# Two adaLN products and their turns move ahead of most of the second tile's first chunks, with identity matmuls between the chunks

## The reference, cut to what matters

```
mod = silu(c) @ w_ada + b_ada             # (1024 x 6144), one row for the prompt, 8 for the samples
shift1, scale1, gate1, shift2, scale2, gate2 = split(mod, 6)
h = rms_norm(x, g_norm1) * (1 + scale1) + shift1
z = h @ w_in                              # one projection of 1024 to 5712 columns
... two attention mixers, gates, w_o_a, w_o_b, w_out, a second norm, and an MLP of width 4096
```

## Time and profile before

| | |
|---|---|
| median of 3 runs | 958.31 us (956.93 to 959.46) |
| profiled execution, its own time | 959.45 us |
| its span, first to last instruction | 957.6 us |
| PE busy | 931.5 us (97%) |
| DVE, ACT, POOL busy | 497.5, 396.5, 140.5 us |
| mean granted TensorE clock | 0.985 of full speed |

### The profile page before, as it was taken

How to read it: one execution, slowest core, us unless ns; L and a number is a source line. 1 busy time by engine, 2 the same in 40 slices (tenths; PEclk the granted TensorE clock), 3 DMA queues, 4 the chain that set the end, 5 groups by cost and what they waited for, 6 DMA issues and landing times.

```text
span 957.6 us, 19787 instructions
## 1 busy us (share of the span) xinstructions
PE 931.5 (97%) x7510; PEld 852.7 (89%) x7510; DVE 497.5 (52%) x1178; ACT 396.5 (41%) x829; POOL 140.5 (15%) x140
## 2 busy tenths in 40 slices
PE   8889999999999999999999999999999999999997
PEld 7588678778888878998799999999999999999997
DVE  2563668964735688742157666444323354442332
ACT  3254646664666756433233434343212143332111
POOL 4200232141244665300000000000000000000000
PEclk9789999999999999999999999999999999999999
DMA  9636683454423555777323611333333333333312
GB/s 318 209 90 193 170 278 95 146 166 131 145 78 120 166 183 154 240 224 242 111 67 89 176 45 45 89 88 91 106 90 88 88 88 89 95 99 90 88 44 90
DMA packets 176233, 124.54 MB, mean 130 GB/s; under 512 B 14739, under 2 KB 152019, under 8 KB 176164
## 3 DMA queue, kind: packets, MB, share of 16 engines
q1 hardware_dynamic: 176034, 123.50, 42.6%
q10 hardware_dynamic: 130, 0.10, 0.0%
HBM read 116.99 MB, written 6.59 MB: 129 GB/s over the span
## 4 chain that ended last, share of the span: by engine, by line
PE 85%; DVE 5%; issue 4%; ACT 2%; POOL 1%; DMA 1%; SPq 0%; POOLq 0%; ACTq 0%; DVEq 0%
PE bank L978 24%; PE bank L979 23%; PE bank L980 22%; PE bank L1053 2%; PE bank L1076 2%; PE bank L1032 2%; PE bank L1062 2%; PE bank L881 1%; PE bank L1094 1%; DMA vbuf<-in_cache_v_a 1%; PE bank L903 1%; PE bank L1038 1%; PE bank L1117 1%; DVE sel L1997 1%; PE bank L1107 1%
## 5 line engine op out<-in xcount | busy, mean ns | idle before, releaser
L978 PE MATMUL bank<-h_hi,w_hi 128*128 128x256 f32 (+1 forms) x1232 | 360.9, 293 | 7.2 <-DVE h_lo L1876 6.5
L979 PE MATMUL bank<-h_lo,w_hi 128*128 128x256 f32 (+1 forms) x1232 | 351.4, 285 | 0.0
L980 PE MATMUL bank<-h_hi,w_lo 128*128 128x256 f32 (+1 forms) x1232 | 350.9, 285 | 0.0
L978 PEld LDWEIGHTS bank<-h_hi,w_hi 128*128 128x128 f32 x1232 | 235.9, 191 | 30.4 <-issue 21.4
L979 PEld LDWEIGHTS bank<-h_lo,w_hi 128*128 128x128 f32 x1232 | 235.8, 191 | 0.0
L980 PEld LDWEIGHTS bank<-h_hi,w_lo 128*128 128x128 f32 x1232 | 235.2, 191 | 0.0
L978 PE MATMUL bank<-u_hi,w_hi 128*128 128x264 f32 (+1 forms) x512 | 145.0, 283 | 0.0
L979 PE MATMUL bank<-u_lo,w_hi 128*128 128x264 f32 (+1 forms) x512 | 144.7, 283 | 0.0
L980 PE MATMUL bank<-u_hi,w_lo 128*128 128x264 f32 (+1 forms) x512 | 144.5, 282 | 0.0
L2414 DVE TENSOR_TENSOR w_lo<-raw,w_hi 128x1024 fp32r<-128x1024 f32 x58 | 71.1, 1226 | 132.9 <-ACT w_hi L1752 132.9
L1752 ACT ACTIVATE w_hi<-raw 128x1024 fp32r<-128x1024 f32 x58 | 61.3, 1056 | 139.8 <-PE bank L980 139.8
(11 more groups left out here) (328 smaller groups left out, 1375.8 us busy)
## 6 DMA issues: line engine op xcount, KB each, us to landing
raw<-in_w_in SPq DMA_DIRECT2D x44, 512.0 KB, 4.1
part<-in_w_ada SPq DMA_DIRECT2D x32, 512.0 KB, 5.8
raw<-in_w_up SPq DMA_DIRECT2D x32, 512.0 KB, 4.1
raw<-in_w_down SPq DMA_DIRECT2D x32, 512.0 KB, 4.2
ada<-in_w_ada SPq DMA_DIRECT2D x4, 2048.0 KB, 13.6
kv<-in_cache_k_b SPq DMA_DIRECT2D x16, 256.0 KB, 4.2
qbc<-q_d SPq DMA_DIRECT2D x16, 256.0 KB, 4.9
kv<-in_cache_k_a SPq DMA_DIRECT2D x16, 256.0 KB, 4.3
```

The lines of the kernel that those rows point to most:

```text
L978: mm(out, hi[:, k, :], x_h, start=first and k == ks[0], stop=False)
L979: mm(out, hi[:, k, :], x_l, start=False, stop=False)
L980: end = mm(out, lo[:, k, :], x_h, start=False, stop=last and k == ks[-1])
```

## The change

On PE, `turn_x(7)` goes to bank 5 in place of bank 2 (so it waits for nothing new, and `mod_product(2)` no longer waits for the store of x chunk 7), `warm(8)` follows it, and `first_tiles` is written in another order: tile 0's chunks 0 to 3, each followed by `warm(2)`; `mod_product(2)` and `mod_product(3)`; tile 1's chunks 0 and 1; `mod_turn(2)` and `mod_turn(3)`; tile 1's chunks 2 and 3; `warm(6)`; then chunks 4 to 7 of both tiles as before. Since bank 5 now holds x chunk 7, tile 1 waits for its store (`xt_dve >= 4`). On DVE, `rest_w(1)` moves from within `first_half(0)` to just behind it. The layout of `w_out` and everything behind `first_tiles` stay as they are.

```diff
-        X_BANK = [0, 1, 4, 5, 0, 1, 4, 2]
+        X_BANK = [0, 1, 4, 5, 0, 1, 4, 5]
...
             def turn_x(j, ts=range(QB)):
                 if ts[0] == 0:
-                    if j == 7:
-                        pe.wait_ge(mod_row_ready, 1)
-                    elif j >= 4:
+                    if j >= 4:
                         pe.wait_ge([xt_act, xt_dve][j % 2], (j - 4) // 2 + 1)
...
             def mod_product(t):
                 if t >= 2:
                     pe.wait_ge(mod_row_ready, t - 1)
-                if t == 2:
-                    pe.wait_ge(xt_dve, 4)
...
             turn_x(7)
+            warm(8)
...
             def first_tiles():
 
-                for tile_ in range(2):
-                    pe.wait_ge(hi_ready, tile_ + 1)
-                    pe.wait_ge(lo_ready, tile_ + 1)
-                    for k in range(4):
-                        pe.wait_ge(h_lo_ready, k + 2)
-                        for half in range(2):
-                            half_tile(tile_, half, half_bank(half + 4 * par(tile_), half), ks=[k], first=k == 0, last=False)
-                    mod_product(2 + tile_)
+                def chunk(tile_, k):
+
+                    pe.wait_ge(h_lo_ready, k + 2)
+                    for half in range(2):
+                        half_tile(tile_, half, half_bank(half + 4 * par(tile_), half), ks=[k], first=k == 0, last=False)
+
+                pe.wait_ge(hi_ready, 1)
+                pe.wait_ge(lo_ready, 1)
+                for k in range(4):
+                    chunk(0, k)
+                    warm(2)
+                mod_product(2)
+                mod_product(3)
+                pe.wait_ge(hi_ready, 2)
+                pe.wait_ge(lo_ready, 2)
+                pe.wait_ge(xt_dve, 4)
+                chunk(1, 0)
+                chunk(1, 1)
                 mod_turn(2)
                 mod_turn(3)
+                chunk(1, 2)
+                chunk(1, 3)
+                warm(6)
                 for k in range(4, NCH):
...
                         rest_h(nrm0, j - 1, at + j % 4 + 1)
-                    if j == 1:
-                        rest_w(1)
                 rest_h(nrm0, 4 * f + 3, at + 5)
...
             first_half(0)
+            rest_w(1)
             store_x(7)
```

## The result

| | before | changed |
|---|---|---|
| median of the first comparison, 9 runs each | 958.61 us | 951.46 us (949.52 to 955.19) |
| profiled execution, its span | 957.6 us | 948.5 us |
| mean granted clock of that execution | 0.985 | 0.994 |

What follows compares the result with a forecast made beforehand. PE was taken as the bound, busy 97% of the span, with three `h_lo` waits and two slow-clock stretches in the opening. Clock 5.0 plus reordering 0.9 gave 5.9 us, so 959.45 - 5.9 = 953.6, range 952.4 to 956.6.

Steps and rivals of the forecast that it cites:

- the sum's chain: Over DVE and ACT, from the start of `mod_turn(3)` to that of chunk 4: 3.92 us, putting chunk 4 at 49.56.
- rival 3: Behind tile 2's start, something later (SP's issues, index scores on DVE) takes half the gain back: 956.5 us, chance 0.06.
- Rivals 2 and 4: First chunks: clock low 34.70 to 41.50, 956.6, chance 0.08; up to tile 2: low clock doesn't recover, 963.2, chance 0.04.
- Rival 1: Behind the two turns of 9 columns the clock falls once more, costing 1.6 to 3.0 us: 955.2 to 956.6, chance 0.32.
- The stage: PE's stretch from the end of the turns of x to tile 2's first matmul: 29.9 us before, predicted 5.9 us shorter.
- the sum: PE's pieces added up from the turns of x (31.40) to tile 2, which starts at 55.40 in place of 61.32.
- 959.45 - 5.9 = 953.6: Whole kernel: the profiled execution's time less the 5.9 us by which tile 2 starts earlier gives the predicted time.
- the first term: Whole kernel: the profiled execution's 959.45 us, 1.14 more than the median of the three, as the base of the forecast.
- rival 5: Whole kernel: the profiled execution's 1.14 us above the median come from outside these slow stretches, median 952.4 us, chance 0.06.
- 5.0 of its 5.9 us hang on the clock: Slow stretches 35.97 to 41.50 and 52.96 to 58.60 at full clock bring 5.0 us; the reordering by itself 0.9.

Runs made afterwards that it cites:

- The last version: Changed kernel without the four pairs of warm-ups and with tile 1's chunk 1 between the two turns: medians 949.89 and 949.87 us, ratios 0.9936 and 0.9932.

## Why the prediction was right or wrong

**What held.** The direction and the place. Both slow windows of the earlier trace rows are gone, chunk 4 starts 3.92 us behind the start of `mod_turn(3)` (the sum's chain was 3.92, and `warm(6)` ended with it), tile 2 starts at 55.00 in two traces where the forecast had 55.40, `store_x(7)` and the move of `rest_w(1)` cost nothing, `warm(8)` ended ahead of the first rest, and the part behind tile 2 took nothing back (rival 3). Rivals 2 and 4 did not occur in any of the three traces of the changed kernel. Rival 1 didn't either, but it is real: the clock fell behind the two turns in the traces without `warm(8)` and with the five early warm-ups, two of the eleven with that order. The bank change was not run by itself. In the trace of before it has nothing to win: the last turn of x starts at 30.60, right behind the piece from 30.44, and `mod_product(2)` at 40.17, after the store that it waited for (37.80 to 38.48).

**The term that was mis-sized.** The stage: 23.5 us where the sum gave 24.0. A pair of warm-ups with the next chunk takes 1.16 us (32.22 from 31.07, and alike behind it), not 1.24; the two products side by side 3.57, not the 3.8 with both change-overs; the starts of the two turns lie 1.33 apart, not 1.44. Together with 0.1 more for tile 1's chunks and for chunks 4 to 7 these are the 0.5 us.

**The step that failed.** "959.45 - 5.9 = 953.6", and the range under it. The sum is a difference, and I hung it on one execution that lies 1.9 us above the mean of what are now 70 runs; hung on that mean, it gives 951.7. That this comes so near the measured 951.46 is partly luck. The forecast lay 2.1 us too high: 1.9 from the execution that it hangs on, 0.9 because the first comparison's median lies that far below the mean of all runs of the changed kernel (952.39), and 0.7 the other way, because the gain is 5.2 by the means over all runs and not 5.9. I saw 1.14 us of the first term (the distance from the median shown) and gave it 0.06 as rival 5, which also set the range's low end. Rival 5's condition is what the traces show: the stage takes 29.92 to 30.06 us in all three traces of before, so its spread comes from elsewhere. The runs show that single executions of one kernel spread from 954.3 to 962.2 (before) and from 949.5 to 955.2 (changed), and mostly with the clock: the seven executions of before with a mean granted clock of 0.988 took 954.30 to 954.85, the four with 0.980 took 960.61 to 961.08. In the traces it is low-clock stretches ahead of the stage and far behind it that come and go. In the first comparison the nine runs of before have a mean of 958.80, 1.2 us above that of all their runs, and the nine of the changed kernel 951.80, 0.6 us below theirs: that takes the 5.2 us of all runs to 7.0. A range that ended 1.2 us under the forecast could not hold such a draw; its end of 952.4 runs through the middle of the changed kernel's runs.

**The reading that was wrong.** "5.0 of its 5.9 us hang on the clock" fits the traces, but I credited all the warm-ups with it. Only `warm(8)` holds the clock where PE stood still: low in six of six traces without it and in none of eleven with it. The second slow stretch goes by the order, with work that had to be done: it is there in all four traces with the old order, twelve warm-ups or not, and in two of eleven with the new one. The pairs only cost: between versions without them, `warm(8)` is worth 0.9 to 1.4 us of stage (22.64 against 23.55 and 24.07 for the order alone), and the pairs take 0.9 back. So the order alone comes out level with the changed kernel.

**Transposes and the clock.** The window of transposes, with one turn of 9 columns among them, is at 1.00 in the changed kernel too (25.10 to 28.60), and so are the 2.5 us behind it, in which `warm(8)` runs. The Trainium skill (TensorE: Matmul & The Clock Gate, Part 4, PE-mode transpose) has transposes not count as work that holds the full clock. The traces here don't bear that out for the stretch ahead of the stage, and the measurement decides. The Trainium skill (same page, Part 1, The HAM clock gate) also has the number of slow matmuls after a start differ from run to run of one kernel. The traces agree for the start of the program: the first 40 warm-up instructions took 6.21 us in one trace of before and 7.68 in another. The two slow stretches of the stage did not differ like that: 29.92 to 30.06 us with both of them in three traces.

**What stays open.** Traces give the stage 6.4 to 6.6 us; the means over all runs differ by 5.2 (the intervals together leave some 4.4 to 6.0). Untraced executions of the kernel before could have shorter slow stretches, or those of the changed kernel could meet rival 1 at times, but the mean clocks on record speak against that as the main cause. They are 0.9852 over the 61 executions of before that have one on record and 0.9920 over 26 of the changed kernel. The difference, 0.0068 of some 955 us, is 6.5 us of full speed lacking, and the two stretches at half speed in the trace of before (34.70 to 41.50 and about 51.8 to 58.6) lack 6.8. So, if the clock elsewhere is alike on average, nearly all of the low clock that the traces show in the stage is there in the untraced executions too. What takes the remaining 1.2 us or so back stays open.

## What to carry to other kernels

A wait in front of dense matmuls is best filled with work that must be done anyway: here the clock then held in nine of eleven traces, and the work cost nothing extra. Warm-ups pay only in a wait that no such work can fill and that they don't outlast, as `warm(8)` does; between chunks they cost their time in series, and in front of work that has become ready they hold it up once the clock has fallen. Look for small-matmul steps (turns, transposed columns) that stand together with waits between, and put a full chunk between them: that took 0.4 to 0.5 us of waiting out of the stage. And when a sum is a difference, hang it on the mean of many executions and give the range the scatter of single ones, not the distance of one profile from one median.

## What the runs showed of the hardware

Low-clock stretches differ between executions of the same program, ahead of and behind the stage. The last version's first trace has one some 290 us behind the stage (window of that trace):

```profile
341.50:344.50 3.00, 3.00 (x9) 1.50 (x10) 1.36 (x6) 1.15 (x5) 0.86 (x1) 0.50 0.91 314
```

and, of the second trace, one wider window around it:

```profile
338.00:346.00 8.00, 8.00 (x64) 6.58 (x62) 7.18 (x21) 6.18 (x15) 2.85 (x2) 1.00 0.79 255
```

The second trace has none in that place. That execution, with a mean granted clock of 0.997, took 944.68 us, 5.2 us less than the median of its series. The start of a program foretells one of them: as said above, the slow stretch between 22 and 30 us followed in the twelve traces whose first 40 warm-up instructions took 6.46 us or more and in none of the four with 6.43 or less; no run here tells why. And a busy PE is no guarantee: in the version with early warm-ups PE was busy for 3.29 of the 3.67 us from 41.13, more than half of it with the two turns of 9 columns and the rest with chunks, and the clock still fell to 0.56 in the window behind.
